# Two transformer blocks in one program: experts in groups of four, an MLP on unnormed tokens, layers written out, mixers in another order, modulation sums by 32x32 transposes

## The reference

```python
h = rms_norm(x, g_mix_norm); proj = h @ w_in
hm = rms_norm(mlstm_chunkwise(silu(conv(m_qk)), m_v, gates)) * sigmoid(m_o)      # 4 heads, 64/128
ha = rms_norm(moba_attention(rope(rms_norm(aq)), rope(rms_norm(ak)), av))        # 4 heads of 64
hl = rms_norm(causal_attention(lora(cq), lora(ckv)))                             # 4 heads of 96/64
x = x + concat(hm, ha, hl) @ w_out
x = x + square(relu(rms_norm(x, g_mlp_norm) @ w_up)) @ w_down                    # 1024 -> 4096 -> 1024
```

```python
mod = silu(c) @ ada_w[i] + ada_b[i]; sh1, sc1, g1, sh2, sc2, g2 = split(mod, 6)
h = rmsnorm(x) * (1 + sc1) + sh1; x = x + g1 * mixers(h)
h = rmsnorm(x) * (1 + sc2) + sh2
x = x + g2 * sum over the token's experts e: gate_e * ((silu(h @ w_gate[e]) * (h @ w_up[e])) @ w_down[e])
```

## Time and profile before

| | us |
|---|---|
| median of 3 runs (lowest, highest) | 2393.95 (2393.73, 2396.99) |
| the profiled execution | 2390.58 |
| its span | 2389.0 |
| PE / VectorE / ScalarE / GpSimd busy | 2130.4 / 972.0 / 375.3 / 86.2 |
| mean granted clock | 0.935 |
| read from HBM | 590.74 MB |

### The profile page before, as it was taken

One profiled execution on the slowest core, in us unless ns is written; L12 is line 12 of the kernel. 1 busy time (PEld: TensorE's weight loads), 2 busy tenths in 40 slices (PEclk: granted clock), 3 DMA queues, 4 the chain that ended last, 5 costly groups with the idle time before them and its releaser, 6 DMA issues.

```text
span 2389.0 us, 23408 instructions
## 1 busy us (share of the span) xinstructions
PE 2130.4 (89%) x8158; PEld 1165.2 (49%) x8158; DVE 972.0 (41%) x2089; ACT 375.3 (16%) x809; POOL 86.2 (4%) x168
## 2 busy tenths in 40 slices
PE   6878999789789998859999999979986999999996
PEld 4555666446466667633333333347664433333332
DVE  3253552134254406847677666733142211111112
ACT  2320001113110001011111111111231111111111
POOL 1111110010011000000000000000000000000000
PEclk9969999899799999979999999998968999999999
DMA  6314885232178742416999999953312599999994
GB/s 230 131 62 170 313 290 181 100 124 106 36 269 307 253 166 106 174 41 282 398 395 404 408 398 396 398 208 106 141 71 73 215 408 397 397 397 397 396 398 183
DMA packets 109511, 592.65 MB, mean 248 GB/s; under 512 B 16647, under 2 KB 21254, under 8 KB 84870
## 3 DMA queue, kind: packets, MB, share of 16 engines
q1 hardware_dynamic: 96390, 541.48, 57.0%
q0 software_dynamic: 13056, 50.33, 6.0%
HBM read 590.74 MB, written 1.05 MB: 248 GB/s over the span
## 4 chain that ended last, share of the span: by engine, by line
PE 69%; issue 22%; DVE 6%; POOL 2%; ACT 1%; DVEq 0%; POOLq 0%; ACTq 0%
PE bank L971 28%; PE bank L698 8%; PE bank L711 7%; PE bank L874 6%; PE bank L961 5%; PE bank L984 5%; PE bank L895 3%; PE bank L1059 1%; PE bank L992 1%; POOL rstd L589 1%; PE bank L1092 1%; PE bank L1007 1%; DVE work L1987 1%; DVE work L1985 1%; PE bank L719 1%
## 5 line engine op out<-in xcount | busy, mean ns | idle before, releaser
L971 PE MATMUL bank<-ring,work 128*64 128x512 f32 x3072 | 673.3, 594 | 32.3 <-DVE work L1987 25.1
L971 PEld LDWEIGHTS bank<-ring,work 128*64 128x64 f32 x3072 | 243.8, 137 | 438.0 <-issue 406.9
L1970 DVE SCALAR_TENSOR_TENSOR work<-work 128x512 f32<-128x512 f32 x384 | 257.3, 745 | 5.7 <-DVE work L1967 5.7
L698 PE MATMUL bank<-hT,ring 128*128 128x256 f32 x1024 | 223.8, 379 | 2.0 <-ACT hT L1142 2.0
L711 PE MATMUL bank<-ring,work 128*128 128x512 f32 x512 | 222.0, 592 | 0.0
L698 PEld LDWEIGHTS bank<-hT,ring 128*128 128x128 f32 x1024 | 194.4, 190 | 35.1 <-issue 9.5
L711 PEld LDWEIGHTS bank<-ring,work 128*128 128x128 f32 x512 | 97.3, 190 | 121.6 <-issue 121.5
L1672 DVE SCALAR_TENSOR_TENSOR work<-ring,cond,work 128x512 f32<-128x512 f32 x168 | 126.3, 752 | 29.6 <-DMA ring<-in_ada_w 23.9
L874 PE MATMUL bank<-hT,ring 128*128 128x256 f32 x608 | 133.9, 383 | 1.5 <-ACT hT L1255 1.5
L656 PE MATMUL bank<-ring,hT 128*128 128x512 f32 (+1 forms) x320 | 133.7, 578 | 0.0
L961 PE MATMUL bank<-work 128*128 128x512 f32 x272 | 127.8, 593 | 1.6 <-ACT work L1322 1.6
(11 more groups left out here) (353 smaller groups left out, 1861.6 us busy)
## 6 DMA issues: line engine op xcount, KB each, us to landing
ring<-in_moe_w_gate SPq DMA_DIRECT2D x64, 2048.0 KB, 8.2
ring<-in_moe_w_up SPq DMA_DIRECT2D x64, 2048.0 KB, 11.7
ring<-in_moe_w_down SPq DMA_DIRECT2D x64, 2048.0 KB, 12.7
ring<-in_ada_w POOLq DMA_DIRECT2D x48, 1024.0 KB, 5.9
ring<-in_w_up SPq DMA_DIRECT2D x16, 2048.0 KB, 8.8
ring<-in_w_down SPq DMA_DIRECT2D x16, 2048.0 KB, 7.8
ring<-in_w_in SPq DMA_DIRECT2D x10, 2048.0 KB, 8.3
ring<-in_cd_w_in SPq DMA_DIRECT2D x6, 2048.0 KB, 7.9
```

The source lines that it names most:

```text
L698: last = pe.matmul(B(4 + b)[:, (c % 2) * S:(c % 2) * S + S], w[:, k, c * P:c * P + P], hT[:, k, :], start=(k == 0), stop=(k == DT - 1))
L971: last = pe.matmul(b[h, :], x[:, k, h], w[e][:, k, c0:c0 + 512], start=(k == 0), stop=(k == kk - 1))
L1970: mo.do(dve.scalar_tensor_tensor(fl(bias[:, h]), mask_b, rbt[:, bass.ds(12 * bk + h, 1)], fl(bias[:, h]), ALU.mult, ALU.add))
```

## The change

What it does, part by part:

- Layers written out: the loop over the first block's layers becomes Python's, so each engine has both layers as straight code.
- Raw-token MLP: PE turns xres itself after the residual. The squares, sums and power run as before, their result squared (rr) is multiplied in where the down product's sum is added to x (relu(r h)^2 = r^2 relu(h)^2 for r > 0).
- Mixers re-ordered: see JOBS. The mLSTM broadcast comes before r20, its mask and exponential for all four heads at once, held in the sixth ring slot (mls); its scores after the lora products, the numerators between o0 and o1. heads_ready lets six of eight column groups be turned before the MLA attention is done, and the output product is cut up and put between MLA's transposes and values. The last two groups (mix3) are no job.
- Modulation sums: VectorE turns the 32x32 blocks of ada_acc, sums 32 columns at a time, and one PE product with a matrix of four identities side by side and stacked (same32) adds the four blocks for all 12 chunks, after MLP unit 14. VectorE adds it with the bias, 12 small instructions.
- Experts by four: one gather serves four experts (256 slots) and makes turned rows at once (xn is stationary, pick moves); the loop runs over 8 quads, of which 7 in the Fori and the last written out without a gather. ScalarE drains all of it and the turned hidden rows. pick for the next quad and pickg are made at different places.
- Router weights have a place of their own (wgate, gbc) and are loaded earlier; the router's product comes before the gate row's; two of four banks are cleared before the ranks; clearing ye and pgT goes.

```diff
-JOBS = (["norm%d" % i for i in range(4)] + ["qk0", "qk1", "gate", "r00", "r01", "r10", "r11", "r20", "r21"]
-        + ["aT0", "aT1", "cT0", "cT1", "cT2", "gT", "v0", "v1", "lq0", "lq1", "lkv0", "lkv1", "o0", "o1"]
-        + ["lT%d" % i for i in range(4)] + ["mix%d" % i for i in range(4)] + ["post%d" % i for i in range(4)])
+JOBS = (["norm%d" % i for i in range(4)] + ["qk0", "qk1", "gate", "r00", "r01", "r10", "r11", "r20", "gT", "aT0", "aT1", "r21"]
+        + ["v0", "v1", "cT0", "cT1", "cT2", "lq0", "lq1", "lkv0", "lkv1", "o0", "o1"]
+        + ["lT%d" % i for i in range(4)] + ["mix%d" % i for i in range(3)] + ["post%d" % i for i in range(4)])
...
-            with sp.Fori(0, L1) as l:
+            for l in range(L1):
...
-            def ada_sum(l, c):
-
-                pe.wait_ge(s["ada_acc"], 24 * l + 2 * c + 4)
-                pe.wait_ge(s["ada_drained"], 12 * l + c + 2)
-                pe.matmul(B(6), ones[:, :], ada_acc[:, c % 2, :], start=True, stop=True).then_inc(s["ada_filled"], 1)
+            def ada_sum(l):
+
+                pe.wait_ge(s["ada_red"], l + 1)
+                pe.matmul(B(6)[:, 0:192], same32[:, :], ada_red.rearrange("p c b -> p (c b)"), start=True, stop=True).then_inc(s["ada_filled"], 1)
...
+                pe.wait_ge(s["rows_ready"], l + 1)
+                for h in range(HM):
+                    last = pe.matmul(B(6 + h // 2)[:, (h % 2) * S:(h % 2) * S + S], pickh[:, h, :], rows[4], start=True, stop=True)
+                last.then_inc(s["m_bc"], 1)
...
+                pe.wait_ge(s["qk_act"], l + 1)
+                pe.wait_ge(s["o_done"], 2 * l + 1)
...
+                pe.wait_ge(s["heads_ready"], l + 1)
+                transposes(l, ["mix0", "mix1", "mix2"], lambda c, t: xn[:, t, c * P:c * P + P], 6)
...
+                out_product(0, 0, 0, 0, 4)
+                out_product(0, 0, 1, 0, 4)
                 p_transposes(6 * l + 3, CAUSAL)
+                out_product(0, 1, 0, 0, 4)
                 values(6 * l + 3, CAUSAL, mla_v, o64)
-
+                out_product(0, 1, 1, 0, 4).then_inc(s["out_filled"], 1)
+                unit(l, U_OUT + 1)
+                for t in range(TT):
+                    for hf in range(2):
+                        out_product(1, t, hf, 0, 2)
...
+                pe.wait_ge(s["x_done"], 2 * l + 3)
+                transposes(l, ["post%d" % i for i in range(4)], lambda c, t: xres[:, t, c * P:c * P + P], DT)
...
+                def gather(r):
+
+                    for d in range(4 * r, 4 * r + 4):
+                        b = (X, T)[d % 4 // 2]
+                        for t in range(TT):
+                            last = pe.matmul(b[:, (d % 2) * S:(d % 2) * S + S], xn[:, t, d * P:d * P + P], pick[:, t, :], start=(t == 0), stop=(t == TT - 1))
+                    last.then_inc(m["gathered"], 1)
...
+                def quad(it, more):
+
+                    pa_, pb_ = 2 * it, 2 * it + 1
+                    hidden(it, 0)
+                    pe.wait_ge(m["pickg_ready"], it + 1)
+                    gates_turned(it, 0)
+                    hidden_turned(pa_)
+                    down(pa_, 0)
+                    down(pa_, 1)
+
+                    hidden(it, 1)
+                    pe.wait_ge(m["pg_drained"], pa_ + 2)
+                    scatter(0)
+                    hidden_turned(pb_)
+                    scatter(1).then_inc(m["scattered"], 1)
...
+                    gates_turned(it, 1)
+                    down(pb_, 0)
+                    if more:
+                        pe.wait_ge(m["p_ready"], it + 2 + i)
+                        pe.wait_ge(m["pg_drained"], pb_ + 2)
+                        gather(0)
+                    down(pb_, 1)
+                    if more:
+                        pe.wait_ge(m["xt_drained"], 2 * it + 3)
+                        gather(1)
+                    else:
+                        pe.wait_ge(m["pg_drained"], pb_ + 2)
+                    pe.wait_ge(m["y_drained"], 2 * pb_ + 4)
+                    scatter(0)
+                    scatter(1).then_inc(m["scattered"], 1)
...
+                    with pe.Fori(0, QUADS - 1) as qd:
+                        quad((q + before) * QUADS + qd, True)
+                    quad((q + before) * QUADS + QUADS - 1, False)
...
+                def gathered(it, r):
+                    act.wait_ge(m["gathered"], 2 * it + r + 1)
+                    for d in range(4 * r, 4 * r + 4):
+                        b = (X, T)[d % 4 // 2]
+                        ins = act.activation(xeT[:, d, :], b[:, (d % 2) * S:(d % 2) * S + S], ACT.Identity, scale=gm[:, 2 * i + 1, d:d + 1],
+                                             bias=sh[:, d:d + 1])
+                    ins.then_inc(m["xt_drained"], 1)
...
+                dve.wait_ge(s["m_bc"], l + 1)
+                bc = bank[:, 6:8, :].rearrange("p b (c n) -> p (b c) n", c=2)
+                do(dve.tensor_tensor(mls[:, :, 0:S], bc, spread(smask[:, 0:S], 1, HM), ALU.add))
+                ins = dve.tensor_tensor(mls[:, :, S:3 * P], bc[:, :, P:S], spread(smask[:, S:3 * P], 1, HM), ALU.add)
+                wait()
+                ins.then_inc(s["m_arg"], 1)
...
+                full_squares(l, "post")
+                r = rs(l, "post")
+                do(dve.tensor_tensor(rr, r[:, 0:TT], r[:, 0:TT], ALU.mult))
...
+                    acc = ada_acc[:, c % 2, :]
+                    if 6 <= c < 10:
+                        do(dve.transpose(ada_t.rearrange("p (k i) -> p k i", k=DT), acc.rearrange("p (i k) -> p k i", k=DT)))
+                    else:
+                        do(dve.transpose(ada_t, acc))
+                    wait()
+                    ins = dve.tensor_reduce(ada_red[:, c, :], ada_t.rearrange("p (b i) -> p b i", i=32), AX_X, ALU.add)
...
-                    ins = dve.tensor_tensor(xres[:, t, :], xres[:, t, :], bank[:, 2 * t:2 * t + 2, :].rearrange("p b n -> p (b n)"), ALU.add)
+                    ins = dve.scalar_tensor_tensor(xres[:, t, :], bank[:, 2 * t:2 * t + 2, :].rearrange("p b n -> p (b n)"), rr[:, t:t + 1], xres[:, t, :],
+                                                   ALU.mult, ALU.add)
...
+                def quad(it, qd, base, more):
+                    mo.start(base)
+                    dve.wait_ge(m["pg_filled"], 2 * it + 1)
+                    picks(mo.do, pickg, 4 * qd, True)
+                    mo.wait()
+                    dve.sem_inc(m["pickg_ready"], 1)
+                    bias_of(4 * qd, 0, 6)
+                    gated(2 * it)
+                    bias_of(4 * qd, 6, 12)
+                    upped(2 * it)
+                    if more:
                         dve.wait_ge(m["gathered"], 2 * it + 2)
+                        picks(mo.do, pick, 4 * qd + 4, False)
                         mo.wait()
                         dve.sem_inc(m["p_ready"], 1)
+                    bias_of(4 * qd + 1, 0, 12)
+                    gated(2 * it + 1)
+                    bias_of(4 * qd + 2, 0, 6)
+                    upped(2 * it + 1)
+                    bias_of(4 * qd + 2, 6, 12)
+                    bias_of(4 * qd + 3, 0, 12)
```

More of the change, by code:

```diff
@@ L1014, in moe, with product @@
-                pe.wait_ge(m["y_drained"], 2 * PAIRS * (n + before) + 2)
-                pe.wait_ge(m["pg_drained"], PAIRS * (n + before) + 1)
-                scatter(0)
-                scatter(1)
+                    return last
+                def product(b, x, w, k, kk, c0):
+                    for e in range(2):
+                        h = slice(SLOTS * e, SLOTS * e + SLOTS)
+                        last = pe.matmul(b[h, :], x[:, k, h], w[e][:, k, c0:c0 + 512], start=(k == 0), stop=(k == kk - 1))
+                    return last
@@ new lines, in hidden @@
+                def hidden(it, j):
+                    pr = 2 * it + j
+                    x = xeT[:, :, P * j:P * j + P]
+                    pe.wait_ge(m["y_drained"], 2 * pr + 2)
+                    for b, c, name in ((G, 0, "g_filled"), (U, 1, "u_filled")):
+                        pe.wait_ge(landedM[c], 16 * pr + 16)
+                        pe.wait_ge(landedM[c + 3], 16 * pr + 16)
+                        for k in range(DT):
+                            if c == 0 and j == 0 and k in (0, 4):
+                                pe.wait_ge(m["xt_drained"], 2 * it + 1 + k // 4)
+                            last = product(b, x, (wslot[c], wslot[c + 3]), k, DT, 0)
+                        last.then_inc(m[name], 1)
@@ new lines, in down @@
+                def down(pr, hf):
+                    if hf == 0:
+                        pe.wait_ge(m["at_drained"], pr + 1)
+                        for c in (2, 5):
+                            pe.wait_ge(landedM[c], 16 * pr + 16)
+                    for k in range(4):
+                        last = product((G, U)[hf], aTe, (wslot[2], wslot[5]), k, 4, 512 * hf)
+                    last.then_inc(m["y_filled"], 1)
+                def quad(it, more):
[26 more added lines that the diff above has]
+                    scatter(1).then_inc(m["scattered"], 1)
```

(39 more changed lines are left out.)

546 lines of the change are left out of this document (249 added, 297 removed).

## The result

| | us |
|---|---|
| kernel before, median of the runs beside it | 2394.4 (2393.7 to 2397.0) |
| kernel after, median of four runs | 2249.8 (2239.9 to 2251.0) |
| ratio after / before | 0.9385, 95% interval 0.9358 to 0.9413 |
| profiled execution after: time, span | 2249.7, 2247.7 |
| forecast | 2245, range 2222 to 2286 |

What follows compares the result with a forecast made beforehand. TensorE, busy 89% of the span, was taken as the bound. Savings of 5.7 + 15.9 + 20.0 + 48.6 + 54.8 + 4.1 = 149.1 us from 2390.6, plus 3.4, gave 2245 us, range 2222 to 2286.

Steps and rivals of the forecast that it cites:

- what the low clock stretches: Mixer stage: busy time TensorE would regain once waits no longer slow its clock, 9.3 us a layer, bounds 0 and 11.
- the five that I had priced: Mixers: waits that stay or are new (first drains, last lora column, lT3, mix2, mix3), 6.3 us in all.
- Rival D: Mixers don't pack: waits move to VectorE's in-order queue, half of 48.6 us stays, 2269 us; chance 0.13.
- my other bound: Expert gather: sixteen products of 256 columns take as long as the old gather, instead of 0.3 us less.
- overlapping tails: Quad of experts: 0.4 us saved where wait and LDWEIGHTS tails overlap, taking 60.4 to 60.0 us.
- Rival A: Expert stages: weight reads bound them, half the gain goes, plus 27 us, 2272 us; chance 0.13.
- B: Expert loop: its code is fetched anew at each of 12 jumps, up to plus 68 us, 2313 us; chance 0.09.
- C: Expert loop: code fetch queued behind weights at every jump, plus 157 us, 2402 us, slower than before; chance 0.02.
- Ahead of the experts: Stretch before each stage's first expert product: 2.7 us less in stage one, 1.4 in two, 4.1 together, bounds 0 and 6.

## Why the prediction was right, and where it was off

*Layers written out*: predicted 5.7, the gap shrank by 5.3, alone 6.1. Right, in place and size.

*Raw-token MLP*: PE's transposes start 2.44 us after the output product, predicted 2.5. The gap shrank by 8.9, not 7.95, since the transposes now begin ahead of the low clock: 2.88 us for them in the timeline, 3.67 in the earlier trace rows.

*Modulation sums*: the removal is 10.0 us a layer, exactly: every MLP at full clock took 220.97 against the predicted 221. What the kernel after shows beyond that, 1.8 us a layer, is the low clock at its start, which the sum assumed away.

*Mixers*: the step that was mis-sized, in my favour. I took 9.3 us for what the low clock stretches, bounds 0 and 11. At full clock the stage is 157.37 us and PE is busy for 149.57 of it, against 167.27 for the same products. So the low clock had stretched the stage by 17.7, above my upper bound. The 7.8 us of waits that are left look like the 6.3 predicted only by luck: heads_ready, which I had put at nothing (12 us of VectorE's work beside 13 of PE's), is the largest with 3.2, and the five that I had priced come to 4.6. That the forecast of 24.3 a layer nearly came out, with 24.9 and 25.5, is luck too: 4 to 6 us of dips were still there. Rival D is out: the stages take 161.6 and 163.0 us, where it asked for over 175, and VectorE holds PE up only at heads_ready.

*Experts by four*: predicted 60.0, measured 60.34, 27.4 against 24.9 a stage. The mis-sized term is the gather. I priced 32 records by the up product's 0.219; they took 3.65 / 16 = 0.228, 7.3 us in all, so nothing was gained over the old gather (my other bound). The waits (0.50 + 0.69 + 0.88 = 2.07) were as predicted (2.2). The 0.4 us for overlapping tails no row or run shows; with the gather and the waits as measured it would have had to be 0.3. Rival A is out at 60.34, but its bound is only 1.6 us away. B and C are out: no instruction packet in 386 us of the loop, and no gap at its jump back. So of the two statements of the Trainium skill that the prediction set against each other (Runtime: NRT & Kernel Launch, Instruction fetch mechanics) the trace bears out the one that gives PE room for 2048 instructions, for a body of 504 records.

*Ahead of the experts*: 5.5 for 4.1. *Left out of the sum*: the stretches of unchanged code, 3.2 us longer in the second block. The mean clock rose in the mixers; what the 3.2 us come from I did not separate.

So 149.1 predicted and 141 measured between the two profiled executions: experts 5.0, MLP 3.8 and layers 0.4 short, unchanged code 3.7 longer, against 5.1 more from mixers, gaps and the stretch ahead of the experts. The 8 us short became 4.8 by luck: I added 3.4 us because the profiled execution before was faster than its median, and that of the kernel after was not (2249.7 and 2249.8).

## What to carry to other kernels

When a matmul-bound kernel has idle stretches, price them twice: the idle time, and the busy time at half clock behind them. Products that nobody reads can remove much of the latter; count their records before sizing them, and first look whether another engine sets the pace there, as VectorE does in the attention. Look for waits on more than is needed (both banks' drains for one product) and for work that can cover the others: three waits of a quad were worth 19 us here, against 50 for the regrouping. And before explaining a difference of half a per cent, compare the same code in several kernels: here it differed by that much by itself.

## What the runs showed of the hardware that was not expected

Equal code, the whole first block, took 799.8, 806.4, 812.5 and 812.7 us in the profiled executions of four kernels, with the mean granted clock of layer 1's mixers at 0.98 in the first and 0.94 in the last two. A loop of 504 matmul records of PE a pass ran with no instruction packet in 386 us. Straight code beside a full weight stream was not faster than the loop: most quads took the same 60.34 us, three took 61.1. A 32x32 transpose of 128x512 on VectorE took 0.71 us, with a stride in the source 1.10.
